# A chunked recurrence on dense operands: 64x64 matmul tiles, one head per quadrant, and chunks pipelined over three neighbours

## What is computed

```python
def rwkv_scan(s0, r, decay, k, v, kk, a, reverse, emit):
    def step(s, inp):                                  # s: heads x 64 x 64
        s_kk = einsum('bhvk,bhk->bhv', s, kk_t)
        s = (s * w_t[:, :, None, :]
             - s_kk[..., None] * (kk_t * a_t)[:, :, None, :]
             + v_t[..., None] * k_t[:, :, None, :])
        y = einsum('bhvk,bhk->bhv', s, r_t) if emit else None
        return s, y

for d in range(2):                                     # forwards, backwards
    s_c, _ = rwkv_scan(0, r_c, w_c[d], kd_c[d], v_c, kk_c, a_c[d], d == 1, False)   # 256 context tokens
    _, y_d = rwkv_scan(s_c, r_x, w_x[d], kd_x[d], v_x, kk_x, a_x[d], d == 1, True)  # 512 latent tokens
    y = y + y_d
```

## Time and profile before

| | us |
|---|---|
| three runs | 4560.47, 4560.58, 4565.48 (median 4560.58) |
| the profiled execution | 4565.88 |
| its span, first to last instruction | 4564.2 |
| recurrent stage within it, first lora product to last state update | 2841.2 to 3704 |
| one context chunk / one latent chunk | about 68 / about 74 |
| busy in the whole span: PE, DVE, ACT, POOL | 3872.1, 1965.1, 1166.3, 916.4 |
| mean granted TensorE clock | 0.882 of 2.4 GHz |

### The profile page before, as it was taken

How to read it: one execution, slowest core, us unless ns; L and a number is a source line. 1 busy time by engine, 2 the same in 40 slices (tenths; PEclk the granted TensorE clock), 3 DMA queues, 4 the chain that set the end, 5 groups by cost and what they waited for, 6 DMA issues and landing times.

```text
span 4564.2 us, 47570 instructions
## 1 busy us (share of the span) xinstructions
PE 3872.1 (85%) x16420; PEld 2668.7 (58%) x16420; DVE 1965.1 (43%) x2791; ACT 1166.3 (26%) x1564; POOL 916.4 (20%) x513
## 2 busy tenths in 40 slices
PE   7998888778489989999997665888888889869996
PEld 6875555433134448782554443878888864357775
DVE  2101445488710021101102334655656641169997
ACT  4321444232210014311001221111111110136663
POOL 4442000000000014430000001000111100049996
PEclk9999999889799999999996555888888879979998
DMA  2224111111012212226111000000000002259996
GB/s 100 96 88 180 46 41 41 35 53 58 20 60 78 74 64 92 92 92 236 64 56 34 12 28 7 1 0 1 0 0 0 0 24 78 101 204 362 357 355 241
DMA packets 106810, 395.88 MB, mean 87 GB/s; under 512 B 11680, under 2 KB 11696, under 8 KB 106112
## 3 DMA queue, kind: packets, MB, share of 16 engines
q1 hardware_dynamic: 95040, 347.42, 21.6%
q0 software_dynamic: 8400, 35.61, 2.1%
q10 hardware_dynamic: 3312, 12.06, 0.7%
HBM read 362.01 MB, written 33.03 MB: 87 GB/s over the span
## 4 chain that ended last, share of the span: by engine, by line
PE 66%; DVE 21%; issue 8%; ACT 3%; DVEq 1%; DMA 1%; POOL 1%; ACTq 0%; SPq 0%; POOLq 0%; PEldq 0%
PE psum L1434 9%; PE psum L827 7%; PE psum L196 5%; PE psum L198 5%; PE psum L197 5%; DVE er_r L1940 5%; PE psum L459 4%; DVE mem L775 4%; PE psum L1003 4%; PE psum L1758 2%; PE psum L1152 2%; PE psum L909 2%; PE psum L469 1%; PE psum L1134 1%; PE psum L834 1%
## 5 line engine op out<-in xcount | busy, mean ns | idle before, releaser
L186 POOL TENSOR_TENSOR ring_r<-ring,whi 128x1024 fp32r<-128x1024 f32 x132 | 319.2, 2437 | 924.9 <-ACT whi L181 924.9
L1434 PE MATMUL psum<-mem 128*128 128x128 f32 x3520 | 463.4, 296 | 4.4
L1434 PEld LDWEIGHTS psum<-mem 128*128 128x128 f32 x3520 | 447.2, 210 | 16.9 <-DVE mem L1614 11.5
L1940 POOL TENSOR_TENSOR er_r<-er,eh 128x1024 fp32r<-128x1024 f32 x134 | 426.4, 3219 | 51.0 <-ACT eh L1928 51.0
L1940 DVE TENSOR_TENSOR er_r<-er,eh 128x1024 fp32r<-128x1024 f32 x134 | 368.1, 2786 | 0.0
L196 PE MATMUL psum<-ffn_xh,ring_r 128*128 128x512 f32 x704 | 279.3, 397 | 24.7 <-DVE xn_r L210 24.7
L681 PE MATMUL psum<-xn,ring 128*128 128x512 f32 x512 | 238.1, 629 | 69.1 <-ACT mem L717 64.7
L197 PE MATMUL psum<-ffn_xh,whi 128*128 128x512 f32 x704 | 281.3, 400 | 0.0
L198 PE MATMUL psum<-xn_r,whi 128*128 128x512 f32 x704 | 279.3, 397 | 0.0
L1928 ACT ACTIVATE eh<-er 128x1024 fp32r<-128x1024 f32 x268 | 261.1, 1072 | 8.1 <-DMA er<-experts 7.2
L681 PEld LDWEIGHTS psum<-xn,ring 128*128 128x128 f32 x512 | 103.1, 203 | 204.1 <-issue 198.9
(11 more groups left out here) (466 smaller groups left out, 6797.1 us busy)
## 6 DMA issues: line engine op xcount, KB each, us to landing
ring<-stream SPq DMA_DIRECT2D x359, 512.0 KB, 3.2
er<-experts SPq DMA_DIRECT2D x276, 512.0 KB, 5.6
xs_dram<-zero_row POOLq DMA_DIRECT2D x1, 12288.0 KB, 38.6
xs<-xs_dram SPq DMA_DIRECT2D x23, 512.0 KB, 6.1
ys_dram<-y_t ACTq DMA_DIRECT2D x23, 512.0 KB, 5.8
mem<-rpb POOLq DMA_DIRECT2D x8, 512.0 KB, 4.4
resid<-x_t SPq DMA_DIRECT2D x1, 2048.0 KB, 8.2
spill<-resid POOLq DMA_DIRECT2D x1, 2048.0 KB, 6.6
```

The costliest lines, as they stand in the source:

```text
L186: pool.tensor_tensor(ring_r[:, s, :, :], ring[:, s, :, :], f(whi[:, s, :, :]), ALU.subtract).then_inc(w_lo, 1)
L1434: ins = pe.matmul(psum[:, bank, q * n:(q + 1) * n], lhs[:, q, :], rhs if rhs is two_ident else rhs[:, q, :], start=True, stop=True)
L1940: eng.tensor_tensor(er_r[:, at, :], er[:, at, :], f(eh[:, at, :]), ALU.subtract).then_inc(done, 1)
```

## The change

- **Dense operands.** Both directions and 4 pairs of heads of one operand lie in one 128x512 tile (`W8 = 8 * L`): partitions 0 to 63 hold the even heads, 64 to 127 the odd ones, and column block `n` of 64 is direction `n // 4`, pair `n % 4`. No zeros are stored, and the halves of 64 partitions are no longer written apart.
- **Products in quadrants.** `prod` now issues, for each of the 8 blocks, one 64x64 matmul on rows and output partitions 0 to 63 and one on 64 to 127: 16 matmuls for both directions where there were 8 of 128x128. `kT` and `bT`, transposes before, are such products with an identity. Lora products stay 64 rows by 128 columns.
- **DVE, ACT and POOL** work on both directions at once: one 128x512 mask, add or copy out of PSUM per product. `X` and `XT` start as an identity that ACT copies (`unit`), and DVE writes the masked product into it with `copy_predicated` (`chosen`). POOL takes over `tb` from DVE. The sign of `bt` is folded in, so that adds take the place of subtracts. `yacc` is no longer zeroed: the first of the two sums is a copy by ACT.
- **Order.** The loops are unrolled to 12 chunks. While the levels of chunk c run, the state part of chunk c-1 and the pair products of chunk c+1 stand between them, and the lora products of chunk c+1 ahead of them (of c+2 on ACT). `kap`, `rho` and `plast` have three buffers, most others two.
- The masks of `constants` are 64 columns wide where they were 128; the transfer to `shared` is 11 instead of 18 tiles, and the lora weights stand there too.

The core of the diff:

```diff
-                    def prod(name, bank, lhs, rhs, n=P):
-                        for q in Q:
-                            ins = pe.matmul(psum[:, bank, q * n:(q + 1) * n], lhs[:, q, :], rhs if rhs is two_ident else rhs[:, q, :],
-                                            start=True, stop=True)
-                        ins.then_inc(s, 1)
+            ROWS = (slice(0, 64), slice(64, 128))
+            tile_ = lambda v, n: v[:, n * L:(n + 1) * L]
+
+            def prod(bank, *terms):
+                for n in range(8):
+                    for i, (lhs, rhs) in enumerate(terms):
+                        for r in ROWS:
+                            ins = pe.matmul(psum[r, bank, n * L:(n + 1) * L], lhs(n)[r], rhs(n)[r], start=i == 0,
+                                            stop=i == len(terms) - 1, skip_group_check=True)
+                return ins
...
-            for d in range(2):
-                for n in "kap bt kt rho v st".split():
-                    pool.memset(dirs[d][n], 0.0).then_inc(rz, 1)
-            pool.memset(yacc, 0.0).then_inc(rz, 1)
-            pool.memset(reset, 1.0).then_inc(rz, 1)
-            pool.wait_ge(rz, 14)
+            pool.memset(st[0], 0.0).then_inc(rz, 1)
+            pool.memset(reset, 1.0).then_inc(rz, 1)
+            pool.wait_ge(rz, 2)
...
+            def pair_R2(c):
+                W(dve_m, c, "CT")
+                prod(5, (of(bt), of(rho[c % 3]))).then_inc(pe_m.sem, 1)
...
+            def pair_bT(c):
+                W(dve_m, c, "R2" if emits(c) else "CT")
+                prod(5, (of(bt), eye)).then_inc(pe_m.sem, 1)
...
+            def level_XY(c, l):
+                W(dve_l, c, f"ym{l}")
+                if l == 1:
+                    W(dve_m, c, "XT")
+                else:
+                    W(dve_l, c, f"xt{l - 1}")
+                if l < 5:
+                    prod(1, (of(XT[c % 2]), of(Ym))).then_inc(pe_l.sem, 1)
+                prod(2, (of(Ym), of(XT[c % 2]))).then_inc(pe_l.sem, 1)
...
+            for c in range(NCH):
+                more = c + 1 < NCH
+                if more:
+                    lora_pe(c + 1)
+                level_Y(c, 1)
+                if c:
+                    state_G(c - 1)
+                level_XY(c, 1)
+                if c:
+                    state_U(c - 1)
+                level_Y(c, 2)
+                if c:
+                    state_Z(c - 1)
+                level_XY(c, 2)
+                if c:
+                    state_y(c - 1)
+                level_Y(c, 3)
+                if more:
+                    pair_AT(c + 1)
+                level_XY(c, 3)
+                if more:
+                    pair_A(c + 1)
+                level_Y(c, 4)
+                if more:
+                    pair_CT(c + 1)
+                    if emits(c + 1):
+                        pair_R1(c + 1)
+                level_XY(c, 4)
+                if more:
+                    if emits(c + 1):
+                        pair_R2(c + 1)
+                    pair_kT(c + 1)
+                level_Y(c, 5)
+                if more:
+                    pair_bT(c + 1)
+                    pair_vt(c + 1)
+                level_XY(c, 5)
```

More of the change, by code:

```diff
@@ new lines, in pair_copy @@
+            def pair_copy(c, name, bank, dst):
+                act.wait_ge(pe_m.sem, pe_m.at(c, name))
+                act.activation(dst[c % 2], psum[:, bank, :], ACT.Copy).then_inc(act_m.sem, 1)
+            lora_in_act(act, 0)
+            sigmoids(0)
+            decays(0, 0)
+            decays(0, 1)
+            lora_in_act(act, 1)
+            unit(0)
+            pair_copy(0, "AT", 5, AT)
+            pair_copy(0, "kT", 6, kT)
+            pair_copy(0, "bT", 5, bT)
+            pair_copy(0, "vt", 6, vt)
@@ new lines, in state @@
+            def state(c):
+                wait(pe_s, c, "Z")
+                if c and emits(c - 1):
+                    wait(pe_s, c - 1, "y")
+                now, then = st[c % 2], st[(c + 1) % 2]
+                dve.tensor_tensor(then, now, psum[:, 7, :], ALU.add).then_inc(dve_s.sem, 1)
+                wait(dve_s, c, "z")
+                wait(dve_p, c, "pl1")
+                dve.tensor_tensor(then.rearrange("p (n v) -> p n v", n=8), then.rearrange("p (n v) -> p n v", n=8),
+                                  plast[c % 3].unsqueeze(2).to_broadcast([P, 8, L]), ALU.mult).then_inc(dve_s.sem, 1)
@@ new lines, in y_sum @@
+            def y_sum(c):
+                if second_sum(c):
+                    wait(pe_s, c, "y")
+                    for d in range(2):
+                        wait(act_s, 11 - c + 4, f"y{1 - d}")
+                        dve.tensor_tensor(y_chunk(c, d), y_chunk(c, d), half(psum[:, 3, :], d), ALU.add).then_inc(dve_s.sem, 1)
+            logits(0, 0)
+            logits(0, 1)
+            for d in range(2):
+                sigmoid(0, d)
+                cumulate(0, d)
+                exclusive(0, d)
+                key_mix(0, d)
@@ L1657, in rwkv_out_pe @@
         def rwkv_out_pe(pe):
[L1658 to L1659 removed]
+            pe.wait_ge(dve_s.sem, dve_s.end())
             pe.wait_ge(xa.sem, xa.at(0, "sgl"))
```

673 lines of the change are left out of this document (367 added, 306 removed).

## The result

| | us |
|---|---|
| kernel before, four runs | 4560.47 to 4565.48, median 4561.5 |
| changed kernel, four runs | 4151.1 to 4158.67, median 4153.98 |
| ratio | 0.9104, 95% interval 0.909 to 0.9117 |
| span of the profiled execution, before and after | 4564.2, 4149.5 |

The change saves 408 us (difference of the medians), 8.9% to 9.1% by the interval. Further kernels that are given without an interval were run once each. The forecast was 4488; what came is the case I gave 9%, quadrants that overlap (4160).

A forecast was written before the change was run, and what follows sets the result against it. PE's pairs of load and MATMUL were taken to bound the recurrent stage: 677 (quadrant pairs) + 63 (lora) + 53 (waits) = 793 us instead of 863. Then 4565.9 - 70 - 7.8 (earlier start) = 4488 us; range 4155 to 4575.

The forecast's parts named there:

- What bounds the stage: Recurrent stage: PE work bounds it, 10,880 quadrant pairs and 384 lora pairs, plus a hand-over or two per chunk.
- The price of a quadrant pair: PE in the recurrent stage: 62.2 ns for each 64x64 load and MATMUL, 10,880 pairs, 677 us.
- The 32 ns of the queue's arithmetic: PE's queue: its own arithmetic takes 32 ns an instruction, cited as support for 62 ns a pair.
- The other bound, 58 ns by the weights: PE's quadrant pairs: 64 weight columns at 0.84 ns plus 5 ns, about 58 ns a pair at 2.4 GHz.
- much faster rival: PE's quadrant pairs overlap, queue no floor: 31 ns a pair, 337 + 63 + 65 = 465 us stage, 4160 us total; 9%.
- Lora: PE's lora products in the stage: 384 pairs of the old form at 0.165 us, 63 us (44 to 83).
- Waits: PE's remaining waits in the stage: 25 + 5 + 8 + 4 + 11 = 53 us.
- 25 + 5 for the masks: PE waiting for DVE's masks of `CT` and `R2`: 25 us in 8 latent chunks, 5 us in context chunks.
- The start: Ahead of the stage: less zeroing by POOL and no ACT wait for PE's loop, first lora earlier, 7.8 us saved.
- DVE's 260 us: DVE busy for about 260 us, costing nothing; never the bound unless a pair falls below some 25 ns.
- The slower rival: PE's quadrants one after the other at the lower clock: 0.11 us a pair, 5008 us, or about 4736; 21%.
- Gains nothing: PE's quadrant pairs at 66 to 71 ns, by a cost of changing quadrant or form: 4550 to 4580 us; 6%.

## Why the prediction was wrong, point by point

- **What bounds the stage: right.** PE's count of pairs times a price. The counts, 10,880 and 384, are those of the trace.
- **The price of a quadrant pair: wrong, and the failure.** 62.2 ns forecast, 29.3 measured at the upper level and 31.8 over the stage with its stretches at the lower one: 346 us of busy time (390.0 - 43.9 of lora) instead of 677, 331 less, in a miss of 334. The step that failed is "I read this as the pace at which PE's queue hands over a load and a MATMUL, and as the floor for any small pair". It rested on one row of one form at one clock level. It was taken for a floor of the queue and for any pair, overlapped or not; the runs show a queue that hands over a pair in 15 ns or less, and two quadrants by turns at half the price of one. The 32 ns of the queue's arithmetic were no support: such an instruction is not a load or a MATMUL.
- **The other bound, 58 ns by the weights: right** as the price of one quadrant alone (59.1). It needed halving for two that overlap, which the much faster rival did.
- **Lora: 63 us forecast, 43.9 measured**, since the clock was up for all groups but the first and a part of the third (6.27 and 3.78 us, the others 3.39): 0.100 us a pair, not 0.165. The lower end of the range, 44, was it.
- **Waits: 53 forecast, 69 measured**: 25 + 5 for the masks came as 22.2 (1.38 us, not 1.6, at 16 places instead of 16 + 4); the first chunk's 8 as 8.0 on `bt` and 1 or 2 on its masks; `bt` was missed (25 us beside the first); the 11 us of wait instructions cost nothing that shows, as 480 pairs with all their waits keep 29.2 ns. The four hand-overs at the end came as 3.9. The rival's 65 was close.
- **The start: right**, 7.8 us forecast, about 8.4 measured.
- **DVE's 260 us: right** (267). That it would cost nothing was wrong: it was called the bound only below some 25 ns a pair, but its order made PE wait already at 29. The POOL products, costed at nothing for their cover, were not hidden from DVE: they lengthened its steps.
- **The slower rival** did not come with this order, but both of its conditions were real, and not independent: without the overlap the clock stayed down, 4781 us. I had joined "quadrants don't overlap" and "lower clock" as two failures that are both needed, as if independent; the runs with the quadrants apart show them together.
- **The much faster rival**: stage 465 forecast, 459 measured; 4160, and 4154 came. Its mechanism is what the runs show; that it came within 6 us is in part luck, since its terms missed by +9 (pairs, 337 and 346), -19 (lora) and +4 (waits). Its chance, 9%, was too small. The argument for it was in the prediction: the 62 ns were something of the small products' own. I held the one row for a floor because nothing in the trace was faster; but no series in it had fewer than 128 weight columns and few moving ones (the loads of 2 columns in the earlier trace rows go with 512 moving). The range's low end, 4155, lies 1 us above the median that came.
- **"Gains nothing"**: its sum was off. 66 ns a pair gives 4529 us, not 4550; the rival was in any case far from what came.

## What to carry to other kernels

At 2.4 GHz and with up to 64 moving columns, a float32 matmul with 64 rows and 64 outputs costs 59 ns a pair alone and 29 to 30 if matmuls on the other half of rows and partitions stand next to it on the queue, so let the quadrant be the innermost loop, with turns of at most four pairs; the same holds for 64 x 128 tiles (100 to 56 ns). Before a row is taken for a floor, ask what it would be at the other clock level and whether any term of its own, here 128 weight columns, explains it as well. When PE's work halves, look at which short steps of DVE it now waits for: moving seven of them in each latent chunk (five in a context chunk) brought 49 us.

## What the runs showed of the hardware that I had not expected

- The clock level does not follow from how busy PE is. With PE busy 96 to 97% of the stage it was granted 0.50 throughout with one quadrant at a time and with 128 x 128 weights and 64 moving columns, and 0.94 to 0.97 with two quadrants by turns (busy 85%) and with 128 moving columns (93%). The order of the same 11,264 pairs alone made the difference between 459 and 1083 us. Nor does the form alone decide: the same 96 pairs of 128 x 128 with 64 moving columns (L1650 above) ran at 1.2 GHz, 20.74 us, as long as the clock had not risen, and at 2.4 GHz, 10.93 us, once the two quadrants by turns had run. What exactly raises it stays open.
- Two quadrants by turns cost 53.5 ns a pair even at 1.2 GHz, less than one quadrant at 2.4 (59.1).
- Two row groups wrote the same PSUM bank, on other partitions, at full pace. The Trainium skill, TensorEngine Tiling (Array Packing), "Gotcha 1: PSUM Pressure", says that row tiles cannot access the same bank simultaneously; the stage's trace shows 29.3 ns, half of one quadrant's 59.1, in one and the same bank, so on other partitions it does not bind.
- Four quadrants by turns reach 15.0 ns a pair. The stage cannot use it as it is laid out: the even heads' results must come out on the even heads' partitions. A layout that could was not tried.
